# First pair of each FFN block as eight plain products by token halves, with the norm ahead of it by halves

## What is computed

```python
D_MODEL = 1024
SEQ = 128
DEC_SEQ = 512
D_FF = 2816
def _rmsnorm(x, gain):
    xf = x.astype(jnp.float32)
    y = xf * lax.rsqrt(jnp.mean(xf * xf, axis=-1, keepdims=True) + EPS)
    return (y * gain.astype(jnp.float32)).astype(x.dtype)

def _swiglu(h, w_in, w_out):
    g, u = jnp.split(h @ w_in, 2, axis=-1)
    return (jax.nn.silu(g) * u) @ w_out
```

## Time and profile before

| | before |
|---|---|
| median of three runs | 2574.25 us (2573.88 to 2576.55) |
| profiled execution | 2577.47 us, of it the span of the trace 2575.7 us |
| mean granted TensorE clock | 0.966 |
| busy: TensorE | 2438.8 us, 95% |
| busy: VectorE | 1520.5 us, 59% |
| busy: ScalarE | 947.5 us, 37% |

### The profile page before, as it was taken

The page is one execution under the profiler, slowest core; times in us unless marked ns, Lnnn a source line. Parts: engine busy times, 40 slices in busy tenths (PEclk is TensorE's granted clock), DMA queues, the critical chain, the costliest instruction groups (busy, mean ns, idle before and its releaser), DMA issues.

```text
span 2575.7 us, 40615 instructions
## 1 busy us (share of the span) xinstructions
PE 2438.8 (95%) x17100; PEld 2334.0 (91%) x17100; DVE 1520.5 (59%) x2397; ACT 947.5 (37%) x1438; POOL 0.2 (0%) x4
## 2 busy tenths in 40 slices
PE   6899999989798999999979999998998988999998
PEld 5899999989487899999979999998998988999998
DVE  6755646647857655646576465564334658647473
ACT  5432423324645433424354243333122235424242
POOL 0000000000000000000000000000000000000000
PEclk8999999989899999999989999998996999999999
DMA  6533543221102524524333252232220012322222
GB/s 231 160 127 123 153 142 123 90 74 50 36 18 67 179 96 139 175 90 128 110 114 124 94 188 89 64 101 64 94 68 10 1 33 66 99 66 89 76 78 78
DMA packets 252175, 251.66 MB, mean 98 GB/s; under 512 B 14978, under 2 KB 246362, under 8 KB 251994
## 3 DMA queue, kind: packets, MB, share of 16 engines
q1 hardware_dynamic: 251994, 249.08, 30.3%
HBM read 245.76 MB, written 3.28 MB: 97 GB/s over the span
## 4 chain that ended last, share of the span: by engine, by line
PE 83%; DVE 9%; ACT 4%; DMA 2%; issue 2%; SPq 0%; DVEq 0%; ACTq 0%
PE banks L830 71%; PE banks L938 2%; DMA w_raw<-ffn_w_in 1%; PE banks L1039 1%; PE banks L1041 1%; PE banks L1040 1%; DVE w_lo L1920 1%; ACT prob L1771 1%; PE banks L1115 1%; DVE z L1989 1%; ACT z L1530 1%; PE banks L1343 1%; PE banks L975 1%; DVE w_raw L1941 1%; DMA mod_grain<-w_mod 1%
## 5 line engine op out<-in xcount | busy, mean ns | idle before, releaser
L830 PE MATMUL banks<-b_hi,w_hi 128*128 128x320 f32 x2464 | 780.9, 317 | 47.2 <-DVE work L2144 17.8
L830 PE MATMUL banks<-b_lo,w_hi 128*128 128x320 f32 x2464 | 769.2, 312 | 0.0
L830 PE MATMUL banks<-b_hi,w_lo 128*128 128x320 f32 x2464 | 768.9, 312 | 0.0
L830 PEld LDWEIGHTS banks<-b_hi,w_hi 128*128 128x128 f32 x2464 | 470.1, 191 | 84.2 <-issue 68.2
L1482 ACT ACTIVATE w_hi<-w_raw 128x1024 fp32r<-128x1024 f32 x308 | 324.4, 1055 | 473.7 <-PE banks L830 308.2
L1920 DVE TENSOR_TENSOR w_lo<-w_raw,w_hi 128x1024 fp32r<-128x1024 f32 x308 | 376.8, 1224 | 192.2 <-ACT w_hi L1482 190.3
L830 PEld LDWEIGHTS banks<-b_lo,w_hi 128*128 128x128 f32 x2464 | 470.5, 191 | 0.0
L830 PEld LDWEIGHTS banks<-b_hi,w_lo 128*128 128x128 f32 x2464 | 470.0, 191 | 0.0
L830 PE MATMUL banks<-hid_hi,w_hi 128*128 128x320 f32 x1664 | 379.5, 309 | 0.0
L830 PE MATMUL banks<-hid_hi,w_lo 128*128 128x320 f32 x1664 | 379.2, 309 | 0.0
L830 PE MATMUL banks<-hid_lo,w_hi 128*128 128x320 f32 x1664 | 379.2, 309 | 0.0
(11 more groups left out here) (282 smaller groups left out, 2594.8 us busy)
## 6 DMA issues: line engine op xcount, KB each, us to landing
w_raw<-ffn_w_in SPq DMA_DIRECT2D x176, 512.0 KB, 4.8
mod_grain<-w_mod SPq DMA_DIRECT2D x256, 256.0 KB, 5.4
w_raw<-ffn_w_out SPq DMA_DIRECT2D x64, 512.0 KB, 4.4
w_raw<-ffn_w_out SPq DMA_DIRECT2D x32, 384.0 KB, 3.8
w_raw<-w_in_odd SPq DMA_DIRECT2D x20, 512.0 KB, 4.8
mod_first<-w_mod SPq DMA_DIRECT2D x4, 2048.0 KB, 16.4
w_raw<-w_in_even SPq DMA_DIRECT2D x12, 512.0 KB, 5.0
w_raw<-w_out_even SPq DMA_DIRECT2D x8, 512.0 KB, 4.1
```

The lines of the kernel that those rows point to most:

```text
L830: ins = pe.matmul(o, w3[w], v3[v][cols], start=first and i == 0, stop=last and i == 2, skip_group_check=onto_read)
```

## The change

The two mixers, the pairs 1 to 10 and the output units but the last two compute as before. What changes:

- **Pair 0 of each block** is eight plain products by token halves (`first_double`, in the opening `opening_double`): half 0 over all eight channel tiles, then half 1, with the raw weights. It has four weight items (`PLAIN_ITEMS`) and no weight sums. Gate and value lie in banks of their own and are gated from there (`sum_forms`).
- **The token sums** t1, t2, z22 - z12 and z21 - t2, first wanted in pair 1, are formed as whole quadrants of 1280 columns in `sum_forms`, behind the split of the plain forms. The raw halves of the weights are free after items 1 and 3, so that the loads for pair 1 may be issued after the splits of these.
- **Norms by halves** (`tail_norm`, `norm_by_half`, `mix_norm`). The sum over channels is a product of ones (128x128) and a half of `ss`, which leaves the sum on every partition (`half_sums`); root and reciprocal work on 128x320 in place. `scale_half` multiplies by the inverse alone, and the shift (`shift_half`) takes the modulation's scale and shift as two pointers. The separate spreading and L1505 go. In the opening both halves are summed, rooted and inverted one after the other.
- **The last two output units** ahead of norms 1 to 5 are cut by halves: (6, half 0), (7, half 0), (6, half 1), the sums of half 0, (7, half 1) (`out_tail`, `tail_pair`).
- **The first two units of both mixers** are interleaved by halves (`fresh_token_units`, `fresh_pairs`).
- **Grains**: the first set of each block is spread over pairs 1 to 3, none beside a norm or in pair 0. In the opening SP loads the modulation's first piece 1 between the two weight halves.

The core of the diff:

```diff
...
-        FIRST_STEPS = [(0, 3), (0, 5), (1, 1), (1, 3), (1, 5), (2, 1), (2, 3), (2, 5)]
-        GRAIN_STEPS = (steps_of(*FIRST_STEPS),
+        GRAIN_STEPS = (steps_of((1, 1), (1, 3), (1, 5), (2, 1), (2, 3), (2, 5), (3, 1), (3, 3)),
                        steps_of((4, 1), (4, 3), (4, 5), (5, 1), (5, 3), (5, 5), (6, 1), (6, 3)),
                        steps_of((7, 1), (7, 3), (7, 5), (8, 1), (8, 3), (8, 5), (9, 1), (9, 3)))
-        ROWS_STEP = ((3, 0), (6, 4), (9, 4))
-        TURN_STEP = ((3, 1), (6, 5), (9, 5))
-        KEEP_STEP = ((3, 2), (6, 6), (9, 6))
+        ROWS_STEP = ((3, 4), (6, 4), (9, 4))
+        TURN_STEP = ((3, 5), (6, 5), (9, 5))
+        KEEP_STEP = ((3, 6), (6, 6), (9, 6))
...
-            def item_step(f, t, k):
-
-                if k == 0:
+            def plain_part(f, hf, k, g, s):
+
+                t = 2 * (k // HK) + g
+                if hf == 0 and k % HK == 0 and s == 0:
                     pe.wait_ge(lo_ready, in_ev(f, 0, t) + 1)
-                    if t == 3:
-                        pe.wait_ge(p5_kept, 22 * f + 1)
-                if t == 0 or t == 1 or t == 2:
-                    pe.wait_ge(form_lo[t], form_done(f, t, k))
-                for s in range(2):
-                    if k == 0 and t == 3 and s == 1:
-                        pe.wait_ge(p5_kept, 22 * f + 2)
-                    ins = item_part(0, t, s, k)
-                    if k == HK - 1:
-                        ins.then_inc(first_part if s == 0 else w_used, 1)
-
...
+                if s == 0:
+                    if k >= HK:
+                        pe.wait_ge(form_lo[2 + hf], HK * f + k % HK + 1)
+                    elif hf == 0:
+                        pe.wait_ge(form_lo[0], HK * f + k + 1)
+                    else:
+                        pe.wait_ge(form12_lo, HK * f + k + 1)
+                hi, lo = plain_form(k, hf)
+                q, cols = in_slot(0, t), slice(s * P, (s + 1) * P)
+                ins = split_product([(bank[PLAIN_BANKS[hf][g][s]][:, 0:HALF], slice(None))],
+                                    (ring_in(w_hi, q)[:, k % HK, cols], ring_in(w_lo, q)[:, k % HK, cols]), (hi, lo),
+                                    k == 0, k == KT - 1)
+                if hf == 1 and k % HK == HK - 1 and s == 1:
+                    ins.then_inc(w_used, 1)
+                elif k == KT - 1:
+                    ins.then_inc(first_sum, 1)
+
+            def plain_parts(f, hf, ks, gs):
+
+                for k in ks:
+                    for g in gs:
+                        for s in range(2):
+                            plain_part(f, hf, k, g, s)
+
+            def first_double(f, n):
+
+                plain_parts(f, 0, range(2), range(2))
+                half_sums(n, 1)
+                plain_parts(f, 0, range(2, KT), range(2))
+                plain_parts(f, 1, range(KT), range(2))
+
+            def opening_double(late_mod):
+
+                plain_parts(0, 0, range(HK), range(2))
+                late_mod(0)
+                plain_parts(0, 1, range(2), (0,))
+                late_mod(1)
+                plain_parts(0, 1, range(2, HK), (0,))
+                late_mod(2)
+                plain_parts(0, 0, range(HK, KT), range(2))
+                plain_parts(0, 1, range(HK), (1,))
+                plain_parts(0, 1, range(HK, KT), (0,))
+                plain_parts(0, 1, range(HK, KT), (1,))
...
+            def half_sums(n, hf):
+
+                pe.wait_ge(square_added, half_squares(n, hf))
+                if hf == 1:
+                    pe.wait_ge(rms_ready, 2 * n + 1)
+                pe.matmul(bank[SUM_BANK][:, 0:HALF], ones[:, :], ss[:, half_of(hf)], start=True, stop=True)\
+                    .then_inc(sums_ready, 1)
+
+            def out_part(f, c, u, hf):
+
+                n, q = CHUNKS[c], out_slot(c, u)
+                for k in range(n):
+                    ins = split_product([(bank[out_banks(u)[hf]][:, 0:HALF], (slice(None), half_of(hf)))],
+                                        (ring_out(w_hi, q, n)[:, k, :], ring_out(w_lo, q, n)[:, k, :]),
+                                        (hid_hi[:, k, :], hid_lo[:, k, :]), k == 0, k == n - 1)
+                return ins
+
+            def out_tail(f, c, n):
+
+                for u in (KT - 2, KT - 1):
+                    pe.wait_ge(lo_ready, out_ev(f, c, u) + 1)
+                    pe.wait_ge(x_updated, out_base(f) + KT * c + u - 1)
+                    out_part(f, c, u, 0).then_inc(tail_part, 1)
+                out_part(f, c, KT - 2, 1).then_inc(w_used, 1)
+                half_sums(n, 0)
+                out_part(f, c, KT - 1, 1).then_inc(w_used, 1)
...
+                for kt in range(KT):
+                    if kt == 2:
+                        half_sums(1, 1)
+                    pe.wait_ge(h_lo_ready, mixed(0, kt, 0))
+                    products(0, 0, kt, 0)
+                    if kt == 0:
+                        pe.wait_ge(x_updated, out_base(1) - KT)
+                    products(0, 1, kt, 1)
+                pe.wait_ge(lo_ready, units[1] + 1)
+                for kt in range(KT):
+                    for t in range(2):
+                        products(1, t, kt, 2 + t)
+                for kt in range(KT):
+                    pe.wait_ge(h_lo_ready, mixed(0, kt, 1))
+                    for t in (2, 3):
+                        products(0, t, kt, 2 + t)
...
+            def root(n, hf):
+
+                act.wait_ge(sums_ready, 2 * n + hf + 1)
+                act.activation(ss[:, half_of(hf)], bank[SUM_BANK][:, 0:HALF], ACT.Sqrt, scale=1.0 / D,
+                               bias=eps[:, 0:1]).then_inc(rms_ready, 1)
+
+            def shift_half(n, view, kt, hf):
 
                 l, j = divmod(n, N_SUB)
-                root(n)
-                keep_ctx_inverse(n)
+                act.wait_ge(scaled_ready, scaled_done(n, kt, hf))
+                for v, cols in HALF_PIECES[hf]:
+                    ins = act.activation(view[:, cols], view[:, cols], ACT.Identity, scale=mod_col(v, l, 3 * j + 1, kt),
+                                         bias=mod_col(v, l, 3 * j, kt))
+                ins.then_inc(z_ready, 1)
+                act.wait_ge(z_ready, scaled_done(n, kt, hf))
+
+            def tail_squares(n, x_before, between, after_first):
+
+                sqrt_table()
+                for d in (KT - 2, KT - 1):
+                    square_half(n, d, 0, x_before)
+                between()
+                root(n, 0)
+                square_half(n, KT - 2, 1, x_before)
+                for kt in range(2):
+                    after_first(kt)
+                square_half(n, KT - 1, 1, x_before)
...
+            def norm_by_half(n, f, x_before, between):
+
+                tail_squares(n, x_before, between, lambda kt: form_high(n, f, kt, 0))
+                for kt in range(2, HK):
+                    form_high(n, f, kt, 0)
+                root(n, 1)
+                item_hi(f, 0, 2)
+                item_hi(f, 0, 3)
+                for kt in range(HK, KT):
+                    form_high(n, f, kt, 0)
+                for kt in range(KT):
+                    form_high(n, f, kt, 1)
+                sum_forms(f)
...
+            def invert(n, hf):
+
+                dve.wait_ge(rms_ready, 2 * n + hf + 1)
+                dve.reciprocal(ss[:, half_of(hf)], ss[:, half_of(hf)]).then_inc(inverse_ready, 1)
+
+            def scale_half(n, view, kts, hf):
+
+                dve.wait_ge(inverse_ready, 2 * n + hf + 1)
+                inverse = ss[:, half_of(hf)].unsqueeze(1).to_broadcast([P, kts.stop - kts.start, HALF])
+                dve.tensor_tensor(view, x[:, kts, half_of(hf)], inverse, ALU.mult).then_inc(scaled_ready, kts.stop - kts.start)
+
+            def tail_norm(n, last_half, scale, low, middle):
+
+                add_sq_half(n, KT - 2, 0)
+                add_sq_half(n, KT - 1, 0)
+                middle()
+                last_half(KT - 2)
+                invert(n, 0)
+                scale(slice(0, 1), 0)
+                add_sq_half(n, KT - 2, 1)
+                scale(slice(1, 2), 0)
+                low(slice(0, 1), 0)
+                scale(slice(2, 4), 0)
+                last_half(KT - 1)
+                low(slice(1, 2), 0)
+                add_sq_half(n, KT - 1, 1)
+                scale(slice(4, 6), 0)
+                low(slice(2, 4), 0)
...
+                dve.tensor_tensor(t1[:, :, :], z12_, z11, ALU.subtract).then_inc(t_ready[0], 1)
+                dve.wait_ge(t_ready[0], f + 1)
+                dve.tensor_tensor(t2[:, :, :], z22_, t1[:, :, :], ALU.subtract).then_inc(t_ready[1], 1)
+                for s in range(2):
+                    dve.wait_ge(first_silu, 2 * f + s + 1)
+                    dve.wait_ge(first_sum, 6 * f + 2 + s + 1)
+                    gated(s, 0)
+                weight_sum(f, 1, 0)
+                dve.wait_ge(w_used, in_ev(f, 0, 1) + 1)
+                low(1, t1[:, :, :])
                 item_lo(f, 1, 0)
+                item_lo(f, 1, 1)
```

(32 more changed lines are left out.)

888 lines of the change are left out of this document (481 added, 407 removed).

## The result

| | before | changed |
|---|---|---|
| median | 2574.25 us (5 runs, 2570.4 to 2576.6) | 2551.2 us (5 runs, 2546.9 to 2556.9) |
| ratio | | 0.9914, 95% interval 0.9895 to 0.9934 |
| profiled execution, span | 2577.5, 2575.7 us | 2551.2, 2549.4 us |
| TensorE clock | 0.966 | 0.974 |

The change gains 23 us, and 42 were forecast; the time lies just outside the stated range, 2516 to 2551. On another chip the changed kernel had a ratio of 0.9896 (0.9881 to 0.9911).

The account below looks back on a forecast made before the run. TensorE was taken as the bound, four fifths of the chain. Stage gains 14.2 + 12.1 + 14.5 + 3.2 + 3.1 - 0.9 = 46.2, less 4.2, made 42.0: from 2574.25 to 2532.2 us, range 2516 to 2551.

Parts of the forecast that it names:

- later steps: Four grains leave FFN 1, FFN 2 and the opening each; 2.14 us moves along, late loads cost nothing.
- The cover: Token sums and their copies hide under half 1 and pair 1's first items; if gone, 3 to 5 us a block return.
- the reserve of 4.2: 0.7 us a stage given back for short waits of 0.2 to 0.3 at hand-overs, 4.2 in all.
- The lead: From a norm's half sums through root and reciprocal (2.13) to the first product: 1.95 us of waiting, where 11.57 lay before.
- Half 0: First half of pair 0: k 0 to 3 without waits, 2.4 us before form 4, 0.35 for item 3's low split.
- two slow stretches of 1.4: Products at the lower clock level behind gaps of 2 us or more in pair 0, 1.4 us for each gap.
- the sign: FFN 1's window from last output product to the last of 192 products should read 36 to 38 us.
- B: Hand-overs make half 0's form step 2.11 us, above TensorE's 1.76; 15.5 us in all, 2547.7 us; chance 0.24.
- C: Reciprocal takes about 0.5 us, so the 1.95 wait goes in five stages; 15 us less, 2517 us; chance 0.09.
- D: Form steps run one behind the other at 2.6 us, 57 us on top, 2589 us; chance 0.04.
- E: Pair 1's waits replace pair 0's in full; the time is within 5 us of before; chance 0.03.
- The mixers and the opening: Mixers gain 3.2 and 3.1 us by interleaved units; the opening loses 0.9, with waits of 4.1 and 0.65.

Follow-up runs that it names:

- grains first: On the changed kernel, SP issues grains 3 and 4 of pair 1 ahead of the load of pair 2's first weight half: 2533.0 us, ratio 0.9837.

## Why the prediction was wrong

**The step that failed** is the one on later steps: "SP's loads of grains, now later, stand behind fewer weight loads; I cost that at nothing (up to 1.3 us a block if a grain is late, as one was once)". It was 5.5, 6.1 and 6.8 us a block. The bound was taken from the kernel before, in which pair 1 starts 53 us behind the output products and not 34. The right question was what stands in front of a grain in SP's queue and what frees it: the load of pair 2's first half, freed by the split of item 4 of pair 1. The cover was laid end to end only as far as items 2 and 3 ("wanted at 58", "wanted at 62.5"). These did arrive in time, TensorE waits for no low part there in any trace, and item 4, the one that frees the weights, was left out. The text had named the price of that cover, 3 to 5 us a block, and in FFN 3 it came out as 4.7. Measured in place of the reserve of 4.2: 31.6, of it 23.5 of waits (18.8 for grains, 4.7 in FFN 3; some 2 of such waits were there before). Most of the rest is the products at the lower clock level behind them: the four stretches read 0.99 for 1.00 over some 1700 us.

With that one term taken away (grains first) the time is 2533.0, where 2532.2 was forecast. That is partly luck: the stages did better, by some 6 us (and 5.5 more by the clock of the odd mixer), and pair 1 still costs more than the reserve.

**The lead** was right within 0.1: 1.89 of waiting in FFN 1 and 3, 1.95 forecast. In FFN 2, where it is hidden less, it is 2.79, 0.90 more; the forecast of that stage had 0.6 for it. The rows behind it (name, shape, count, busy, mean ns):

```profile
L2220 DVE RECIPROCAL ss<-ss 128x320 f32<-128x320 f32 x12 | 25.7, 2149 | 4.3 <-ACT ss L1692 4.3
...
L1700 ACT ACTIVATE z_b<-z_b,mod 128x192 f32<-128x192 f32 x24 | 12.8, 534 | 0.0
L1700 ACT ACTIVATE z_b<-z_b,mod 128x128 f32<-128x128 f32 x24 | 11.6, 481 | 6.9 <-DVE z_b L2226 6.9
```

The reciprocal takes 2.149 us, where 2.13 was taken by carrying on from the earlier trace rows. The Trainium skill's rule ("VectorE: DVE Perf Modes", section "First, the fixed hardware budget") had by my estimate given 2.8; the measurement decides against reading it as eight cycles a column. The shift with two pointers takes 481 ns at 128 columns where one with a single pointer took 400. The Trainium skill gives some 93 ns for a pointer ("ScalarE: Activation LUTs", section "What ACT_TABLE_LOAD costs"), and the difference here is 81: the row roughly agrees. A form step was 1.33 to 1.34 on ScalarE, nearer to the 1.36 of the rows than to the 1.55 that the forecast had drawn from that rule.

**Half 0.** The wait at k = 4 was 1.50 for 2.4 forecast, and one of 0.90 at k = 2, behind half sums 1, was not forecast. With the lead these waits are 4.3 us, and 1.95 + 2.4 + 0.35 = 4.7 were forecast. What was mis-sized is the clock: two slow stretches of 1.4 were put into each stage, and the clock in all three pair-0 windows is 1.00. The 2.8 are more than the 2.1 to 2.7 us by which each beat its forecast, and enough for the window of FFN 1 to end at 34.3, below the 36 to 38 that were named as the sign. The rule behind the term, 1.4 for each gap of 2 us or more, did not hold in the rows of before either: at 833.01 the product behind a wait of 3.61 lasts 0.39.

**The rivals.** B's time, 2547.7, is the nearest, but its mechanism did not occur: no wait at every k of half 0. C and D did not occur: the reciprocal was not cheap, and the steps did not run serially. E was right in kind, waits of several us in pair 1, and wrong in size: it took back half of the gain (31.6 of 57.9), not all. It had been given a chance of 0.03 only, because its cause had not been followed to a queue.

**The mixers and the opening** came out near their forecasts, 3.2 and 2.6 (less the clock), and -1.4 for -0.9. In the opening this is luck in part: its two waits for low parts are 7.4 and 4.9 us, and 4.1 and 0.65 stand in the forecast. That the interleaved units are what brings the mixers' gain was not tried by itself.

## What to carry to other kernels

When an engine gets ahead by ten microseconds, follow each buffer that it will want next back to what frees it, and lay that out for one stage more than the one that is changed: here the gain was lost one pair later, at an item that frees a weight half. In a queue that issues in order, a load for which there is a free buffer should not stand behind one that waits for another engine; moving two grains ahead, 1 MB in four loads, gave back 20 us. And an instruction of which only small shapes are on record can be priced by the slope between them, as the reciprocal was here (2.13 for 2.149).
